# Half of one gate's products moved from the sliding attention into the scan, over DRAM

## The reference, cut to what matters

```python
h = rmsnorm(x, norm_mix[i])
proj = h @ w_in[i]
...
gate_a = proj[..., OFF_GATE:OFF_GATE + D_MODEL]
gate_b = proj[..., OFF_GATE + D_MODEL:]
attn = windowed_gqa_sink(q, k, v, attn_sink[i])
ssd = ssd_branch(z, xbc, dt_raw, conv_w[i], conv_b[i], dt_bias[i], a_log[i],
                 d_skip[i], ssd_norm[i])
merged = (jax.nn.sigmoid(gate_a) * (attn @ w_attn_branch[i])
          + jax.nn.sigmoid(gate_b) * (ssd @ w_ssd_branch[i]))
x = x + merged @ w_out[i]
```

## Time and profile before

| | |
|---|---|
| median of 3 runs | 2532.42 us (2531.89 to 2533.18) |
| the profiled execution's own time | 2532.29 us |
| its span | 2530.5 us |
| TensorE (PE) busy | 2467.6 us (98%) |
| VectorE (DVE) busy | 1465.0 us (58%) |
| ScalarE (ACT) busy | 1168.2 us (46%) |
| mean granted TensorE clock | 0.995 of full |

### The profile page before, as it was taken

One profiled execution on the slowest core, in us unless ns is written; L12 is line 12 of the kernel. 1 busy time (PEld: TensorE's weight loads), 2 busy tenths in 40 slices (PEclk: granted clock), 3 DMA queues, 4 the chain that ended last, 5 costly groups with the idle time before them and its releaser, 6 DMA issues.

```text
span 2530.5 us, 35862 instructions
## 1 busy us (share of the span) xinstructions
PE 2467.6 (98%) x14408; PEld 2009.4 (79%) x14408; DVE 1465.0 (58%) x2366; ACT 1168.2 (46%) x2091; POOL 159.5 (6%) x156
## 2 busy tenths in 40 slices
PE   9999999999999999999989999999999999999998
PEld 6888778888777678888867878888877877888886
DVE  6665554433656564344378898877676556543343
ACT  5354353322456644233247676666455444432232
POOL 2110110000100010000000111111000010100001
PEclk9999999999999999999999999999999999999999
DMA  5222234534322223333324333333322233233322
GB/s 155 76 60 76 59 102 113 131 104 119 95 87 82 67 68 106 93 100 90 102 61 142 97 108 114 109 105 121 105 66 67 98 120 100 78 105 100 95 96 75
DMA packets 201782, 243.42 MB, mean 96 GB/s; under 512 B 8081, under 2 KB 133297, under 8 KB 201361
## 3 DMA queue, kind: packets, MB, share of 16 engines
q1 hardware_dynamic: 201616, 241.12, 32.0%
HBM read 231.00 MB, written 9.57 MB: 95 GB/s over the span
## 4 chain that ended last, share of the span: by engine, by line
PE 80%; DVE 11%; ACT 6%; issue 3%; DMA 0%; POOL 0%; DVEq 0%; SPq 0%; ACTq 0%; POOLq 0%
PE bank L1987 23%; PE bank L1989 22%; PE bank L1988 22%; DVE CV L2696 2%; DVE wlo L2471 1%; PE bank L1993 1%; PE bank L1995 1%; PE bank L1994 1%; PE bank L2006 1%; ACT whi L2256 1%; PE bank L2188 1%; DVE h L2505 1%; PE bank L2196 1%; PE bank L2209 1%; PE bank L2101 1%
## 5 line engine op out<-in xcount | busy, mean ns | idle before, releaser
L2471 DVE TENSOR_TENSOR wlo<-raw,whi 128x1024 fp32r<-128x1024 f32 x389 | 489.3, 1264 | 647.6 <-ACT whi L2256 645.1
L2256 ACT ACTIVATE whi<-raw 128x1024 fp32r<-128x1024 f32 x389 | 406.8, 1053 | 580.8 <-PE bank L1989 569.1
L1987 PE MATMUL bank<-XAh,whi 128*128 128x512 f32 x1552 | 616.6, 397 | 6.4 <-DVE XAl L2479 3.4
L1989 PE MATMUL bank<-XAh,wlo 128*128 128x512 f32 x1552 | 602.4, 388 | 0.0
L1988 PE MATMUL bank<-XAl,whi 128*128 128x512 f32 x1552 | 602.3, 388 | 0.0
L1987 PEld LDWEIGHTS bank<-XAh,whi 128*128 128x128 f32 x1552 | 292.3, 188 | 79.0 <-issue 11.8
L1989 PEld LDWEIGHTS bank<-XAh,wlo 128*128 128x128 f32 x1552 | 292.0, 188 | 61.4
L1988 PEld LDWEIGHTS bank<-XAl,whi 128*128 128x128 f32 x1552 | 292.3, 188 | 57.6 <-issue 1.0
L1987 PE MATMUL bank<-XBh,whi 128*128 128x512 f32 (+1 forms) x840 | 331.6, 395 | 1.8 <-DVE XBl L2477 1.7
L1989 PE MATMUL bank<-XBh,wlo 128*128 128x512 f32 (+1 forms) x840 | 324.0, 386 | 0.0
L1988 PE MATMUL bank<-XBl,whi 128*128 128x512 f32 (+1 forms) x840 | 323.8, 385 | 0.0
(11 more groups left out here) (330 smaller groups left out, 3258.7 us busy)
## 6 DMA issues: line engine op xcount, KB each, us to landing
raw<-in_w_in SPq DMA_DIRECT2D x77, 512.0 KB, 4.0
raw<-in_up SPq DMA_DIRECT2D x64, 512.0 KB, 3.7
raw<-in_down SPq DMA_DIRECT2D x64, 512.0 KB, 3.7
raw<-in_a_w_in SPq DMA_DIRECT2D x32, 512.0 KB, 4.1
E<-scr_rows SPq DMA_DIRECT2D x32, 512.0 KB, 5.5
raw<-in_w_up SPq DMA_DIRECT2D x32, 512.0 KB, 3.6
raw<-in_w_down SPq DMA_DIRECT2D x32, 512.0 KB, 3.6
raw<-in_w_kv SPq DMA_DIRECT2D x16, 512.0 KB, 3.6
```

The lines of the kernel that those rows point to most:

```text
L1987: pe.matmul(out, wh[:, w, c], xh[:, x, r], start=st, stop=False)
L1989: m = pe.matmul(out, wl[:, w, c], xh[:, x, r], start=False, stop=en)
L2256: act.activation(s.hi, s.raw, ACT.Copy).then_inc(s.whi[0], 1)
L2471: dve.tensor_tensor(s.lo, s.raw, s.hi.bitcast(F32), ALU.subtract).then_inc(s.wlo[0], 1)
```

## The change

Two of the four tile pairs of the first gate (features 0 to 511) are multiplied in the scan: one behind the four tiles of group 0, one between the second and third tile of group 1. Their tanh goes into temporaries and is stored to a DRAM scratch. At the start of the sliding attention four loads bring the tiles into `MA`, and its loop over the gates leaves these two pairs out. The setup's seven semaphores become two counting ones; the four transfers have one each.

```diff
--- before.py
+++ after.py
@@ -880,7 +880,8 @@
         g0, (tile, ones) = v_gemm(0), norm_sum(8)
         for k in range(8):
             if k == 5:
-                s = add("setup", lam=sig("lam"), lb=sig("lb"), eps=sig("eps"), lam1=sig("lam1"), lam2=sig("lam2"), lb1=sig("lb1"), lb2=sig("lb2"))
+                s = add("setup", eps=sig("setup.dve"), lam1=sig("setup.dve"), lb1=sig("setup.dve"), lam=sig("setup.dve"), lb=sig("setup.dve"),
+                        lam2=sig("setup.act"), lb2=sig("setup.act"))
                 K.lam, K.lb, K.eps = s.lam, s.lb, s.eps
             split(XB, k, hsrc(k), ht[k], scale=col(gain["a_norm_pre"] + k), src2=K.gain_in)
             tile(hsrc(k), ht[k])
@@ -1270,7 +1271,7 @@
 
     KW, VW = ZS0[:, :, :].rearrange("p (a b) d -> p a (b d)", b=2), XT0
     KD = sb("KD", [P, 2, S], scope=both)
-    qk, w_free = {}, {}
+    qk, w_free, kept = {}, {}, {}
 
     def Q_tile(k):
         return CVs[k // 4][:, k % 4, :]
@@ -1464,17 +1465,27 @@
                 XH[bt % 2].open()
                 wdone.add(bt)
 
+        def early_gate(n):
+            def evac(j, i, b, m):
+                k, t = 2 * n + j[1] // P, tmps.take()
+                e = add("gate_a", dst=t.t[:, :], bank=b, unit=m, dst_free=t.after, gate=sig("gate.a"))
+                b.free(e.gate)
+                yield
+                kept[k] = add("gate_store", dst=io["gate_scr"][:, k, :], src=t.t[:, :], gate=e.gate, land=sig(f"gate{k}", 16)).land
+                t.free(kept[k])
+            return two_tiles([(OFF_GATE + n * 256, 256)], evac, gate=lambda: tmps.room(2), ring=unit_ring, piece=2)
+
         def products():
             for g in range(8):
                 if g == 0:
                     act_[:] = [add("spill", dst=io["hs"], src=h[:, :, :], ready=[ht[7], XA.ready[7]], land=sig("spill", 16)).land] * 8
-                for s in ('0123', '0123', '0123z', '0123z', '01a2z3b', '01a2z3b', '01a2z3b', '01a2z3b')[g]:
+                for s in ('0123g', '01g23', '0123z', '0123z', '01a2z3b', '01a2z3b', '01a2z3b', '01a2z3b')[g]:
                     if s in "0123":
                         yield from x_gemm(g, unit_ring, [int(s)])
                     elif s == "z":
                         yield from z_gemm(g, unit_ring)
-                    elif s == "k":
-                        yield from kw_gemm(unit_ring)
+                    elif s == "g":
+                        yield from early_gate(g)
                     else:
                         yield from branch((g - 4) // 2, (g - 4) % 2 * 2 + "ab".index(s))
             for qt in range(4):
@@ -1643,6 +1654,8 @@
         Rt = K.Rt = sb("Rt", [P, 384], scope=sc)
         add("load_rel", dst=Rt[:, :], src=io["relpos"], scope_free=end, land=sig("rel_in", 16))
         K.rel_in = (p.sems["rel_in"], 16)
+        for k in range(4):
+            mt[k] = add("load_gate", dst=MA[:, k, :], src=io["gate_scr"][:, k, :], stored=kept[k], scope_free=end, land=sig(f"gate{k}", 16)).land
         add("act_table", name="exp_and_others")
         SW = Ring([Slot(sb(f"SW{i}", [P, 4, 384], scope=sc)) for i in range(6)])
         stw = sb("stw", [P, 16, 16], scope=sc)
@@ -1672,7 +1685,7 @@
             yield from qw_gemm(2, ring_all, 2)
             yield from qw_gemm(3, ring_all, 2)
             for br in range(2):
-                for n in range(4):
+                for n in range(2 - 2 * br, 4):
                     yield from gate_gemm(n, br)
             XA.open()
             yield from branch_gemm(0)
@@ -2914,6 +2927,14 @@
             for t in s.ready:
                 on.wait_ge(*t)
             sp.dma_start(s.dst, s.src).then_inc(s.land[0], 16)
+        elif k == "gate_store":
+            on.wait_ge(*s.gate)
+            sp.dma_start(s.dst, s.src).then_inc(s.land[0], 16)
+        elif k == "load_gate":
+            on.wait_ge(*s.stored)
+            for t in s.scope_free:
+                on.wait_ge(*t)
+            sp.dma_start(s.dst, s.src).then_inc(s.land[0], 16)
         elif k == "row_store":
             on.wait_ge(*s.copied)
             sp.dma_start(s.dst, s.rows).then_inc(s.land[0], 16)
@@ -2942,7 +2963,7 @@
             sp.wait_ge(sem, plan.sent[name])
 
 
-DMA_SIGNALS = {"gain_in", "cst_in", "tab_in", "bias_in", "rows", "T0", "T1", "dtrows", "E0", "E1", "E2", "E3", "spill", "rel_in", "mem_in", "out"} | {f"{x}{k}" for x in "hx" for k in range(8)}
+DMA_SIGNALS = {"gain_in", "cst_in", "tab_in", "bias_in", "rows", "T0", "T1", "dtrows", "E0", "gate0", "gate1", "gate2", "gate3", "E1", "E2", "E3", "spill", "rel_in", "mem_in", "out"} | {f"{x}{k}" for x in "hx" for k in range(8)}
 
 
 def program(nc, io, out_d):
@@ -2950,6 +2971,7 @@
     io = dict(io)
     io["hs"] = nc.dram_tensor("scr_h", [128, 8, 512], F32, kind="Internal")[:, :, :]
     io["scr_t"], io["scr"] = scr, scr[:, :, :]
+    io["gate_scr"] = nc.dram_tensor("scr_gate", [128, 4, 512], F32, kind="Internal")[:, :, :]
     io["row_scr"] = nc.dram_tensor("scr_rows", [32, 2, S], F32, kind="Internal")
     with ExitStack() as es:
         lens = make_plan(nc, io, out_d, es, None).counts
```

## The result

| | before | after |
|---|---|---|
| median | 2532.74 us of 21 runs (2531.14 to 2533.75) | 2536.63 us of 21 runs (2532.73 to 2539.38) |
| profiled execution, its own time | 2532.29 us | 2538.10 us |
| its span | 2530.5 us | 2536.3 us |

The ratio is 1.0015, with an interval of 1.0009 to 1.0021: 3.9 us slower, clear of zero by its interval though under the 5.1 us that the prediction took as the least to tell, 9.5 us above the forecast and just above the range's end of 2536. The profiled execution of after lies 1.5 us above the median of its runs.

A forecast was written before the change was run, and what follows sets the result against it. TensorE, busy 98% of the span, was taken as the bound, so only its waits and lower clock could be won. -12.7 (scan) + 1.1 (first wait) + 6.4 (tail) = -5.2 us, giving 2527.1 us, range 2521 to 2536.

The forecast's parts named there:

- What bounds the kernel: Whole kernel: TensorE is busy 98% of the span, so only its waits, mostly for `E`, and lower clock can be won.
- the moved products: Two gate pairs, 96 products, leave the sliding attention and enter the scan: +21.9 and -21.9 us.
- What goes in the scan: Scan's front, 1403 to 1545 us: TensorE's waits and clock loss of 14.8 us mostly go, -12.7 us.
- own signs of being wrong: Waits for `E` or a bank among groups 1 to 3, at head 7's scores, or a store ahead of late weights.
- The bound of -6.5: Scan's front, least gain: only the 3.75 us wait and its 2.7 us share of the clock go.
- The first wait: Ahead of group 0's states: 1.84 us wait goes, the next grows from 2.08 to about 4.1; +1.1 us (0 to 2).
- The sliding attention's tail: End of sliding attention: 38 pieces of cover where 43 are needed, leaving head 7 uncovered; +6.4 us (2.5 to 11).
- Nothing for stores, loads and the setup: Moved tanh, four stores, four loads and merged setup signals cost nothing; bounds 0 to +2 us.
- Waits move instead of going: Rival, scan groups 2 and 3: waits 2.59 and 1.05 come back, only 6.5 us goes; 2533.3 us, chance 0.19.
- VectorE sets the front's pace: Rival, scan's front: it lasts as VectorE needs, so gate pairs cost 5.1 us, not 21.9; 2521.9 us, chance 0.12.
- Banks run short: Rival, end of sliding attention: heads 6 and 7 have four banks, +12.6 us on the forecast; 2539.7 us, chance 0.09.
- doesn't do what it says: Rival, scan: planner holds gate pairs back as filler for later in the scan; 2538.7 us, chance 0.04.

The follow-up runs named there:

- scan_only: The change, but the sliding attention still computes all eight gate pairs and loads nothing back; 2555.06 us, 1.0085 of the kernel before.
- tail_only: Kernel before's scan, without early gates; sliding attention omits two gate pairs and loads spilled residual instead (wrong values); 2515.87 us, 0.993 of the kernel before.
- z_earlier: The change, with z moved ahead of the third group's last two tiles and the fourth's last tile; 2531.36 us, 0.9992 of the kernel before.
- first_late_z: The change, with its first pair ahead of group 0's first tile and z earlier in the third and fourth groups; 2524.86 us, 0.9970 of before.
- scan_no_store: The change with all eight gate pairs kept in sliding attention, no loads back and no early gate stores; 2551.97 us, 1.0077 of the kernel before.
- scan_no_store_2: Repeat of the kernel with all eight gate pairs kept in sliding attention, without loads back or early gate stores; 2554.25 us.
- one_mid: Kernel before with one gate pair moved, behind the first group's four tiles; seven pairs stay in the sliding attention; 2535.02 us, 1.0008 of before.

## Why the prediction was wrong

**What bounds the kernel, and the moved products**: right. TensorE's busy time stayed (2468.9 for 2467.6), and scan_only, with 96 products more and nothing gained, took 22.1 us longer. That the waits were *mostly* for `E` was loosely read: 7.3 of 15.3 us between 1361 and 1810.

**What goes in the scan, -12.7**: this step failed. It measured -0.6, from the second `sc_carry` of group 0 to the anchor. Told by waits and clock: the change idles 11.4 us from 1403.4 us to the anchor, where 10.3 were idle before; the clock cost 0.02 x 85.5 = 1.7 us there, for 4.8 (these stretches begin at the same time, not at the same step). What was wrong is how it counted: it set TensorE's steps (transposes, outputs) against the convolutions, by pieces, and found their waits gone, which is so. It did not set the *other* steps of the same chains, the norm, the exponentials of `E` and the state updates on ScalarE and VectorE, against the weight splits. Before, ScalarE's norm of group 0 runs at 1428.6 to 1434.5, when the z products of 1419.65 to 1433 have their weights; after, it runs at 1425.0 to 1433.8, and z is next. "Every step stands eight pieces later at the same place among the products" holds from the anchor on, and for the groups between, from which all the gain was to come, nothing was laid out but TensorE's steps and the convolutions. Of the prediction's own signs of being wrong, waits for `E` or for a bank among groups 1 to 3, that for a bank came (1.59 us); the one for `E` is 1.68, where 1.08 stood before. The others, for z's weights and a weight unit, were on no list. The bound of -6.5 was no bound: it took it as given that a wait that goes is not replaced. That end should have been no gain at all.

**The first wait**: right in place and size (4.52 for about 4.1, the load of `E` used from 1366.71 as before). Products behind the first output stand 1.4 us later against the transposes than before, for +1.1 (0 to 2).

**The sliding attention's tail, +6.4 (2.5 to 11)**: right, a little too high: 5.0 in the change, 4.8 by tail_only; 2.49 us of waits and 1.7 of clock are seen directly. The count of pieces, 38 for 43, also said what one pair would do (42), and one pair cost nothing.

**Nothing for stores, loads and the setup**: right within the spread, though a store landed in 5.2 us and a load back in 4.5 (medians), not in the 2.7 that was taken; tail_only, which has the merged signals and the loads, has the waits of before in the scan, 3.7 and 2.5 us among them, and the anchor 0.5 us later. But SyncE's queue was not idle cover either: in the change ScalarE waits once 5.93 us for `E`, at 1456.53, whose load stood in SyncE's queue behind weight loads until 1450.15; without stores that is 3.59 and 3.02. It is not on TensorE's path there.

**The rivals.** *Waits move instead of going* (2533.3) is what happened, larger than it was priced: it let 6.5 us go for good, and 0.6 went. *VectorE sets the front's pace* fell: from 1403.4 to 1460 it was busy 45.3 of 56.6 us, less than before (48.4), and waited more. By the Trainium skill (Perfetto Trace Analysis, Identifying the Most-Contended Engine) VectorE would have been the engine to relieve in that stretch. No run takes work from VectorE, so none tests that; z_earlier and first_late_z gain 5 and 12 us on the change and leave VectorE the same work. *Banks run short* and *doesn't do what it says* did not come about: no bank wait at scores in the sliding attention, and the pairs stand where the code puts them.

What stays open is why the wait at the fourth group's z is 1 us longer with the stores than without; it doesn't show in the medians of the pairs of runs taken together (2555.06 and 2553.27 with, 2551.97 and 2554.25 without).

## What to carry to other kernels

An idle engine is not always filled by giving it work near its waits. Where engines work strictly in a list's order, added work shifts every chain against every other, and each chain's steps on *all* engines must be laid against the operand preparation that shares those engines, not only those of the engine that waits. Put the filler where it can move nothing, ahead of the chain whose latency it is to cover (here a load that was 4 us late); and count how much cover the place that it is taken from can spare, since 42 pieces for 43 cost nothing and 38 cost 5 us.

## What was not expected of the hardware

**The same wait costs different amounts from execution to execution.** Two profiles of the same kernel, scan_no_store and then scan_no_store_2, have the same five waits within 0.1 us up to 1561 us (4.07 and 3.99 ahead of the first states, 2.93 and 2.95 at the third group's z among them). Two stretches behind these two waits:

```profile
1360.00:1380.00 20.00, 15.93 (x104) 12.85 (x103) 9.07 (x9) 13.59 (x31) 5.12 (x3) 0.91 0.58 185
1430.00:1460.00 30.00, 27.07 (x192) 24.36 (x190) 24.39 (x40) 19.73 (x42) 4.28 (x3) 0.94 0.29 88
```

```profile
1360.00:1380.00 20.00, 16.01 (x69) 12.95 (x68) 9.16 (x10) 14.29 (x32) 5.11 (x3) 0.83 0.58 185
1430.00:1460.00 30.00, 27.05 (x187) 24.73 (x186) 23.05 (x36) 19.16 (x40) 6.46 (x4) 0.89 0.29 88
```

The granted clock (third column from the end) is 0.91 and 0.94 in the one, 0.83 and 0.89 in the other: TensorE stayed longer at its 1.2 GHz level after the same wait. That makes 0.08 x 20 = 1.6 us in the first stretch and 0.05 x 30 = 1.5 in the second. The third group's first z product stands at 1439.92 and 1442.10, the anchor at 1620.90 and 1624.11, 3.2 us apart, of which 0.6 was there before the first stretch's wait ended. So a price of a wait read from one execution is not sure by 1 to 2 us. How far the runs of a kernel spread is not shown to come from that: the change has six waits of over 1.5 us from the first states to the anchor and its 21 runs spread over 6.7 us, but one_mid has five and its 11 runs spread over 1.9.

**VectorE's split took twice as long beside GpSimd.** In z_earlier, VectorE's and GpSimd's timelines at the split that z of the fourth group waits for:

```profile
1477.43 2.28 DVE L2484 TENSOR_TENSOR wlo<-raw,whi 128x1024 fp32r<-128x1024 f32 x1
```

```profile
1476.91 1.71 POOL L2871 TENSOR_TENSOR rr<-CB,cst 128x512 f32<-128x512 f32 x1
```

A split takes 1.22 us elsewhere; GpSimd's product ends at 1478.62, and 1.22 on top of that is 1479.84, the split's end being 1479.71. The Trainium skill (SBUF — State Buffer, SBUF: two separate sides) says that a VectorE instruction with two SBUF inputs and a GpSimd one that reads SBUF take turns at a shared pair of ports, the later one held in full; this pair of rows agrees with it. It made the split 1.06 us longer, with TensorE waiting for it.

Nor is it one pair of rows, or new with the change. In the kernel before, from 1240 to 2200 us, ten splits begin while a GpSimd instruction runs; they take 1.47 to 2.50 us, and each ends 1.07 to 1.09 us after that instruction does, as here (1479.71 for 1478.62). One of them, VectorE and GpSimd:

```profile
1506.19 2.49 DVE L2471 TENSOR_TENSOR wlo<-raw,whi 128x1024 fp32r<-128x1024 f32 x1
```

```profile
1505.68 1.92 POOL L2854 TENSOR_TENSOR xb<-XT,s_ds 128x768 f32<-128x768 f32 x1
```

In these profiles such a split shows as long, not as waiting.
